# Nineteen large and 45 small expert jobs instead of 36 and 28, and the gate/up products of the large jobs in plain fp32

## The reference

```python
scores = jax.nn.sigmoid((h @ router_w).astype(jnp.float32))
biased = scores + router_bias
... # best 4 of 8 expert groups, then the top 8 experts of a token by biased score
w = w / jnp.sum(w, axis=-1, keepdims=True) * ROUTED_SCALE
hg = jnp.einsum('nd,edf->nef', h, e_gate)     # 64 experts, 1024 x 256 each
hu = jnp.einsum('nd,edf->nef', h, e_up)
act = jax.nn.silu(hg) * hu * gates[:, :, None]
routed = jnp.einsum('nef,efd->nd', act, e_down)   # 256 x 1024 each
shared = (jax.nn.silu(h @ s_gate) * (h @ s_up)) @ s_down
```

## Time and profile before

| | us |
|---|---|
| median of 3 runs | 1051.63 (1049.86 to 1051.92) |
| profiled execution | 1049.66 |
| its span, first to last instruction | 1047.5 |
| PE (matmul) busy | 975.9 |
| DVE / ACT / POOL busy | 593.7 / 375.4 / 233.3 |
| first expert `up` to end of the last `down` | about 400 to 1016.8 |

### The profile page before, as it was taken

How to read it: one execution, slowest core, us unless ns; L and a number is a source line. 1 busy time by engine, 2 the same in 40 slices (tenths; PEclk the granted TensorE clock), 3 DMA queues, 4 the chain that set the end, 5 groups by cost and what they waited for, 6 DMA issues and landing times.

```text
span 1047.5 us, 18756 instructions
## 1 busy us (share of the span) xinstructions
PE 975.9 (93%) x6321; PEld 696.1 (66%) x6321; DVE 593.7 (57%) x1346; ACT 375.4 (36%) x613; POOL 233.3 (22%) x172
## 2 busy tenths in 40 slices
PE   2799999999998898999999999999999999999980
PEld 1699999999997775444565655656565655656540
DVE  1656889999767444422445546464545545464517
ACT  3544444434462310112334333342424333242422
POOL 2000000000000001122333434343433434343322
PEclk9899999999999969999999999999999999999995
DMA  9975568687766275699999999999999999999813
GB/s 332 259 226 164 163 183 298 230 283 256 230 231 228 79 324 215 232 317 318 336 389 377 390 374 382 373 376 382 375 370 367 378 353 367 359 373 356 290 20 114
DMA packets 105674, 305.60 MB, mean 292 GB/s; under 512 B 15427, under 2 KB 57539, under 8 KB 80628
## 3 DMA queue, kind: packets, MB, share of 16 engines
q1 hardware_dynamic: 89715, 283.80, 73.2%
q0 software_dynamic: 15408, 19.69, 7.8%
q10 hardware_dynamic: 499, 1.40, 0.4%
HBM read 309.23 MB, written 31.42 MB: 325 GB/s over the span
## 4 chain that ended last, share of the span: by engine, by line
PE 91%; DVE 5%; DMA 2%; ACT 1%; issue 1%; ACTq 0%; SPq 0%; DVEq 0%; POOLq 0%
PE psum L767 36%; PE psum L1067 12%; PE psum L1039 10%; PE psum L1041 10%; PE psum L771 9%; PE psum L1072 5%; PE psum L786 2%; PE psum L957 2%; PE psum L985 1%; DMA bc<-in_norm_g 1%; PE psum L822 1%; PE psum L948 1%; PE psum L1005 1%; DVE wexp_r L1478 1%; DVE wexp L2015 1%
## 5 line engine op out<-in xcount | busy, mean ns | idle before, releaser
L767 PE MATMUL psum<-xn_r,wexp_r 128*128 128x264 f32 x1024 | 192.7, 288 | 2.2 <-DVE wexp_r L1478 2.2
L767 PEld LDWEIGHTS psum<-xn_r,wexp_r 128*128 128x128 f32 x1024 | 161.1, 191 | 4.8 <-DVE wexp_r L1478 2.7
L767 PE MATMUL psum<-hT_r,wexp_r 128*128 128x264 f32 x512 | 146.1, 285 | 0.0
L1884 DVE SCALAR_TENSOR_TENSOR hT<-psum,gcol,hT 128x256 f32<-128x256 f32 x64 | 30.6, 478 | 191.4 <-ACT hT L1372 191.4
L1067 PE MATMUL psum<-wexp,hT 128*128 128x512 f32 x288 | 129.7, 593 | 0.0
L1478 DVE TENSOR_TENSOR wexp_r<-wexp,wexp_r 128x1024 fp32r<-128x1024 f32 x88 | 106.6, 1219 | 27.2 <-ACT wexp_r L1206 26.9
L687 POOL DMA_INDIRECT y_odd<-mT,scatter_row x32 | 73.6, 2299 | 207.1 <-DVE gcol L1851 183.7
L767 PE MATMUL psum<-mod_room_r,mid_r 128*128 128x512 f32 x336 | 119.0, 409 | 0.0
L1039 PE MATMUL psum<-wexp,mid 128*128 128x512 f32 x240 | 110.8, 595 | 0.8 <-ACT mid L1358 0.8
L1206 ACT ACTIVATE wexp_r<-wexp 128x1024 fp32r<-128x1024 f32 x88 | 92.2, 1053 | 50.2 <-PE psum L767 42.5
L1041 PE MATMUL psum<-wexp,mid 128*64 128x256 f32 x448 | 108.6, 385 | 0.0
(11 more groups left out here) (291 smaller groups left out, 1490.7 us busy)
## 6 DMA issues: line engine op xcount, KB each, us to landing
wexp<-in_e_gate SPq DMA_DIRECT2D x64, 1024.0 KB, 8.1
wexp<-in_e_up SPq DMA_DIRECT2D x64, 1024.0 KB, 10.6
wexp<-in_e_down SPq DMA_DIRECT2D x64, 1024.0 KB, 9.6
wexp<-in_w_in SPq DMA_DIRECT2D x32, 1024.0 KB, 6.3
mid<-in_ada_w SPq DMA_DIRECT2D x8, 2048.0 KB, 9.5
wexp<-in_ada_w SPq DMA_DIRECT2D x4, 2048.0 KB, 20.1
wexp<-in_w_branch SPq DMA_DIRECT2D x8, 1024.0 KB, 5.0
wexp<-in_w_out SPq DMA_DIRECT2D x4, 1024.0 KB, 5.9
```

The lines of the kernel that those rows point to most:

```text
L767: last = mm(out, a[x], b[y], start=start and x == y == 0, stop=stop and x == 1)
```

## The change

Only group 0 stays all large; from group 1 on job 0 of a group is large and jobs 1 to 3 are small: 4 + 15 = 19 large and 45 small. The ranks of the jobs follow. No job is split: every large `up` is eight k of plain fp32, and the ACT and DVE work of the split goes. Because more experts may now exceed their slots, the extra pass also runs when more than LARGE = 19 experts have over 64 rows; it goes through the jobs in their sorted order, and a small job's positions are shifted by 64 first. The count of such experts is made at the end of group 0 (`rows_beyond`), and `cnt_i` is written there and no longer before the jobs.

```diff
-LARGE = 2 * UNROLL + (NE - 2 * UNROLL) // 2
+LARGE = UNROLL + (NE // UNROLL - 1)
...
-            return isinstance(i, int) and i < 2 or j % 2 == 0
+            return isinstance(i, int) and i == 0 or j == 0
...
-            g.iota(rank_of_job_i[:, 0:2 * UNROLL], pattern=[[1, 2 * UNROLL]], base=0, channel_multiplier=0)
-            g.iota(rank_of_job_i[:, 2 * UNROLL:], pattern=[[2, NE // UNROLL - 2], [1, 2], [LARGE - 2 * UNROLL, 2]],
-                   base=2 * UNROLL, channel_multiplier=0)
+            g.iota(rank_of_job_i[:, 0:UNROLL], pattern=[[1, UNROLL]], base=0, channel_multiplier=0)
+            ranks = rank_of_job_i[:, UNROLL:].rearrange("p (i j) -> p i j", j=UNROLL)
+            g.iota(ranks[:, :, 0:1], pattern=[[1, NE // UNROLL - 1], [0, 1]], base=UNROLL, channel_multiplier=0)
+            g.iota(ranks[:, :, 1:], pattern=[[UNROLL - 1, NE // UNROLL - 1], [1, UNROLL - 1]], base=LARGE, channel_multiplier=0)
...
                 for k in ks:
-                    if is_split(i, j) and k < KS:
-                        if k % 2 == 0:
-                            pe.wait_ge(S["gu_lo"], pieces_until(i, j, k // 2))
-                        last = mm3(psum[:, j % 2, :].rearrange("p (a f) -> p a f", a=2), [as_r(xg_high[:, k, :]), as_r(x[:, k, :])],
-                                   [as_r(gu_high[:, k]), as_r(w[:, k])], start=(k == 0), stop=(k == KT - 1))
-                    elif is_large(i, j):
+                    if is_large(i, j):
...
-                for p in ps:
-                    F(as_r(gu_piece(gu_high, p)), gu_piece(w_gu[j], p), ACT.Copy).then_inc(S["gu_hi"], 1)
...
-                    V.tensor_tensor(as_r(gu_piece(w_gu[j], p)), gu_piece(w_gu[j], p), as_r(gu_piece(gu_high, p)).bitcast(F32),
-                                    ALU.subtract).then_inc(S["gu_lo"], 1)
...
-            V.tensor_copy(cnt_i[:], cnt_f[:]).then_inc(S["cnt_ready"], 1)
...
+            def rows_beyond():
+
+                link(V.tensor_scalar(keys[:, 1, :], keys[:, 0, :], float(NE * (HALF + 1)) - 0.5, None, ALU.is_gt))
+                link(V.tensor_reduce(cnt_f[:, 1:2], keys[:, 1, :], AX.X, ALU.add))
+                link(V.tensor_scalar(cnt_f[:, 1:2], cnt_f[:, 1:2], float(LARGE) + 0.5, float(TOK), ALU.is_gt, ALU.mult))
+                link(V.tensor_tensor(cnt_f[:, 0:1], cnt_f[:, 0:1], cnt_f[:, 1:2], ALU.max))
+                V.tensor_copy(cnt_i[:], cnt_f[:, 0:1]).then_inc(S["cnt_ready"], 1)
...
+                    if first and j == UNROLL - 1:
+                        rows_beyond()
...
+            def shift_small():
+
+                small = posm_job[:, :, UNROLL:].rearrange("p t (i j) -> p t i j", j=UNROLL)[:, :, :, 1:]
+                V.tensor_scalar(small, small, float(CAP - HALF), None, ALU.add).then_inc(S["x_shift"], 1)
...
-            extra_passes(ve, extra)
+            extra_passes(ve, extra, shift_small)
```

More of the change, by code:

```diff
@@ L286, in in_mid @@
             used[0] += n
-            assert at + n <= 3 * D
+            assert at + n <= 4 * D
             return mid[:, at:at + n]
@@ L441, in bass_decoder_step, with extra_passes @@
         fin_y = wexp[:, 1, :].rearrange("p (a t d) -> p a t d", a=2, t=3)
-        def extra_passes(eng, step):
+        def extra_passes(eng, step, prepare=None):
             eng.wait_ge(S["cnt_ready"], 1)
@@ L449, in extra_passes @@
             with eng.If(longest > CAP):
+                if prepare:
+                    prepare()
                 for r in range(1, ROUNDS):
@@ L574, in _, with extra @@
             load_down(final, UNROLL - 1)
-            def extra(r, e, n):
+            def extra(r, job, n):
                 sp.wait_ge(S["x_xt"], n + 1)
+                e = sp.value_load(order_i[0:1, bass.ds(job, 1)], min_val=0, max_val=NE - 1)
                 for at, view in ((0, gate_v), (2048, up_v), (4096, down_v)):
@@ L1126, in extra @@
                 for t in range(3):
-                    rhs = tab[:, t, :, :].rearrange("p e c -> p (e c)")[:, bass.ds(2 * e, 2)]
-                    last = mm(psum[:, LIST_BANK, 0:2], oh[:, 0, t, :], rhs, start=(t == 0), stop=(t == 2))
+                    rhs = tab_job[:, t, :, :].rearrange("p e c -> p (e c)")[:, bass.ds(LISTC * e, LISTC)]
+                    last = mm(psum[:, LIST_BANK, 0:LISTC], oh_job[:, 0, t, :], rhs, start=(t == 0), stop=(t == 2))
                 last.then_inc(S["x_list"], 1)
@@ L1349, in rows_out @@
                 need(ac, S["up_done"], e - 1)
[L1350 to L1354, removed]
-                    ac.wait_ge(S["xg_hi"], 2 * (2 * (i - FIRST_SPLIT) + j // 2) + 2)
-                    ac.sem_inc(S["xgt_act"], 1)
-                    return
                 F(xgT[j % 2][:, 0:4, 0:n], psum[:, 5, :].rearrange("p (k c) -> p k c", k=4)[:, :, 0:n], ACT.Copy).then_inc(S["xgt_act"], 1)
@@ L1395, in body @@
                     pi, pj = (i if j else i - 1), (j - 1) % UNROLL
-                    ahead = (i if j < 2 else i + 1), 2 - j // 2 * 2
-                    more = not (last and j >= 2)
                     if prev:
                         act_out(pi, pj)
-                    if more and j % 2:
-                        gu_highs(*ahead, (2,))
                     gate_out(i, j)
@@ L1406, in body @@
                         y_out(pi, pj)
-                    if more and j % 2 == 0:
-                        gu_highs(*ahead, (0, 1))
             await_full(ac, ("shared_up", 1))
@@ L1936, in body @@
                     pi, pj = (i if j else i - 1), (j - 1) % UNROLL
-                    ahead = (i if j < 2 else i + 1), 2 - j // 2 * 2
-                    more = not (last and j >= 2)
-                    if more and j % 2:
-                        gu_lows(*ahead, (0, 1))
                     if not prev:
@@ L1945, in body @@
                     keep_scatter_row(i, j)
-                    if more and j % 2:
-                        gu_lows(*ahead, (2,))
                     gated(i, j)
```

49 lines of the change are left out of this document (9 added, 40 removed).

## The result

| | before | after |
|---|---|---|
| median, us | 1051.20 (1049.86 to 1051.92, 4 runs) | 1033.25 (1031.37 to 1034.46, 4 runs) |
| profiled execution, us | 1049.66 | 1032.33 |
| its span, us | 1047.5 | 1030.6 |
| start of the last `down` product, us | 1016.18 | 999.65 |
| from there to the end of the span, us | 31.3 | 31.0 |

The ratio is 0.983, with a 95% interval of 0.9814 to 0.9847. The change saves 18 us. The forecast was 41 (1011), and 1033 lies outside its range of 1001 to 1028.

The account below looks back on a forecast made before the run. PE bounds the kernel, with DMA nearly as full. PE alone would save 48.2 us, but DMA's last landing at 972.4 leaves 40.4: 1049.66 - 40.4 = 1009.3, put at 1011 as runs' median is 2.0 higher; range 1001 to 1028.

Parts of the forecast that it names:

- the DMA part: DMA engines from 460 us on: 518 us of work, 7.6 off for empty slots; last landing 972.4 if kept full.
- The allowance for a backlog: Gate/up loads are issued 26 to 29 us ahead, so 12 to 15 us beyond 13.8 are absorbed before PE stalls.
- Rival (b): Expert stage: no DMA slack, slowest of 16 engines sets each landing, 534 us repeat; saving 21, 1031 us; chance 0.10.
- Its sign did not come: Expert groups: landings reaching 25 us and groups never below 35.5 us would show that DMA has no slack.
- PE's sum: TensorE segments: group of four 33.63 us against 36.24, group 1 35.0; PE alone would save 48.2 us.
- the total of 1003: Whole kernel if PE alone sets the time: 1051.6 - 48.2 = 1003 us.
- (a): Expert stage: PE stays the bound, a deeper backlog lets the engines run without gaps; 1003 us; chance 0.22.
- (d): Expert loop: turn-round of two `y_rows` buffers, `y_out` waiting for scatters, makes it slower: about 1098 us; chance 0.03.
- my 3.5 ns of all engines: Gathers and scatters: price of one empty slot on all 16 engines; 2176 slots fewer take 7.6 us off.
- 518 us of work: DMA engines from 460 to near 994 us: 523.6 us of share, 518 of the 534 at full share 1.01.
- the forecast 8 us of waits: PE between 480 and 980 us: some 8 us idle, released by weight loads, in the first half above all.
- The rule: Weight loads from HBM: by a limit of about 358 GB/s, the 194.6 MB from 460 us on would take 544 us.

Follow-up runs that it names:

- the run with both orders: Kernel after with small jobs' slot order dealt evenly by the packets, run from engine 15 down in jobs 2 and 3 of each group: 1002.94 us (0.9548).
- the run with the first backward orders: Kernel after with the slot order of small jobs 1 and 2 of each group run backwards over the 16 rings: 1025.82 us (0.9766).

## Why the prediction was wrong

**The step that failed** is the one in the DMA part: "The last landing then comes at 460 + 2 + 518 - 7.6 = 972.4 us if the engines are kept full. They are". A deep queue keeps an engine full only if that engine has work left; PE waits for a whole load, and a whole load ends with its slowest engine. By counting weight packets in the trace after, at 566.17 us PE waited for load number 49 from the start of the expert stage while all engines together had moved the bytes of 51.8 loads; at 606.18, for number 61 with 64.9 moved. At the ten waits before a large `up` the mean was 2.8 to 5.3 loads ahead of the load waited for. Where the rows are dealt evenly (the run with both orders) a gate/up load of jobs 12 to 60 lands when the mean is at most 1.0 load ahead. SP cannot issue more until PE frees a slot, so behind each such wait the fast engines run dry, which makes the share of 0.97. The allowance for a backlog fell short too: 12 to 15 us beyond 13.8 were said to be absorbed, and the loads took 28 to 30 us from their issue. The last weight packet ended at 994.1 us in place of 972.4, and PE the last `down` at 1000.2 and not at 976.4.

**Rival (b)** named this mechanism, "because the slowest of the 16 engines sets each landing", and its price of 1031 is 2 us from the result. The mechanism was right; that the price fits is in part luck. It takes the 534 us from 460 to 994 as what the loads need, and in the kernel before those were PE's pace: the order that takes 26 us off the kernel after changes nothing there, and with both orders the same packets end at 958.6 us. Its sign did not come either, for groups did come below 35.5 us (33.35 for group 2). I gave it 0.10, with "shares of 0.98 and 0.93 with landings not growing" against it. Those shares are means over 16 engines and could not speak against an uneven one. What could have spoken was there: in the kernel before the landing of an `e_up` load is 13.8 us, but of the sixteen semaphore increments that make it up (load issued at 595.15) some thirteen come 8.2 to 10 us after the issue, and only the last three at 11 to 13.8. A landing row shows the last of sixteen only.

**Right, and how well.** PE's sum: the group of four 33.35 (33.63 forecast), group 1 34.84 (35.0), the unsplit `up` 1.01 us dearer per large job (27 us for 28 jobs in the run with that alone). The group is 0.28 us too long in the sum, 4 us over 14 groups, so the total of 1003 is some 4 us high; without live rows, and so without waits for loads, the kernel takes 997.37. That the run with both orders took 1002.94, (a)'s time, is a coincidence: it still has 4.1 us of waits for loads, and the clock behind them. And (a)'s reason, a queue deep enough to run without gaps, is not what brought it there. No wait for DVE or a scatter appears, and one of 0.5 us for ACT, so (d) is out, and the tail behind the last `down` is unchanged. Empty slots: my 3.5 ns of all engines for each was not borne out, since 5760 more of them went with a faster run; as the rows were dealt in another way there too, their price stays open.

**A second size that was off.** I read a share of 1.01 as a full pipe and so took 518 us of work for granted. With the rows even, the engines move 404 GB/s at a share of 1.02, against 369 at 0.98 in the kernel before. So a packet takes longer where less is asked of the engines, and a share near 1 overstates the work; this is read from those two rows, no run tests it by itself. By itself this would have made the forecast too slow; it was covered by the larger error in the other direction.

**What I did not price.** The clock behind the waits: beside the 10 waits of 23.4 us the large `up` itself takes 149.3 us in place of 138.6 (the run without live rows), 10.7 more or 46% on top. By that the forecast 8 us of waits would have been 12.

**The rule.** In the best run the core moves 404 GB/s over 197 us, all queues together, and 425 in the pure stream of the trace after (371 to 389 us). The Trainium skill, "DMA: Bandwidth & Descriptors" (Specifications), gives some 358 as the HBM limit of a core, and "HBM Reference" (Specifications) some 425 for a core that streams alone. As the prediction had it, the traces disagree with the first and agree with the second.

## What to carry to other kernels

A transfer over 16 engines is as fast as the fullest of them. Before comparing two nearly equal resources, look at the spread inside the one whose profile row is a mean. Its sign is waits for loads in a stretch whose DMA share falls; close by, the share is full during a wait (1.04) and falls some microseconds behind it (0.70), when the fast engines have run out of work. And an order of rows written for one transfer size is not right for another: read the dealing from the packets before relying on it, since here a single iota pattern was worth more than the whole change (26 us against 18), but only after the change.

## What the runs showed of the hardware

- An indirect transfer of 64 slots and one of 128 deal their slots by different patterns (2 slots of an engine in each half of 32; 4 slots in each of two quarters). This is inferred from packet sequences, and for the 64 slots borne out by 26 us.
- In the kernel after, the six waits of PE of 1.97 to 4.61 us before a large `up` are followed by half an `up` of 5.18 to 6.38 us in place of 3.63 to 3.70, at a granted clock of 0.50 to 0.62 over the 4 us from the end of each: 1.5 to 2.7 us beyond the wait itself. After the four waits of 0.45 to 1.25 us it takes 3.67 to 3.70. The length of the wait alone does not decide: in the run with the first backward orders a wait of 3.06 us (before 719.58) is followed by 3.70 us at a clock of 1.00.
- An empty slot is a packet of 4 or 8 bytes and about 9 ns; a kernel with 5760 more of them was not slower, though its rows were also dealt in another way.
- With the rows dealt evenly the core sustained 404 GB/s from 703 to 900 us, 382 of them on the weight queue (75.20 MB), beside gathers and scatters; 380 in all had looked like a limit.
- An issue on SP's queue stretches from 0.33 to as much as 3.3 us while loads take some 28 us to land.
